# Moving operands placed 256 bytes away from stationary ones, modulo 512, in a two-block kernel on one core

## What is computed

```
first_block, for each of 2 layers:
    h = h + hybrid_mixer(rmsnorm(h))            # ends in y @ w_mix_out
    h = h + cross_attention(rmsnorm(h), mem)    # x @ w_xq, mem @ w_xkv, o @ w_xo
    layer 0:  h = h + swiglu(hn, w_gate, w_up, w_down)             # inner width 2816
    layer 1:  h = h + moe_swiglu(hn, ...)      # 8 experts of inner width 3584, top 2 of 8
second_block: mLSTM and LRU branches, two merges, then a lookup of 16 rows
    for each of 8 heads of each token in a table of 16384 experts
```

## Time and profile before

| what | value |
|---|---|
| median of three runs | 2800.35 us |
| the profiled execution | 2810.22 us |
| its span, first to last instruction | 2808.5 us |
| TensorE busy | 93% of the span |
| VectorE busy | 71% |
| ScalarE busy | 42% |
| mean granted TensorE clock | 0.968 of full speed |
| bytes moved by DMA | 776.22 MB |

### The profile page before, as it was taken

One profiled execution on the slowest core, in us unless ns is written; L12 is line 12 of the kernel. 1 busy time (PEld: TensorE's weight loads), 2 busy tenths in 40 slices (PEclk: granted clock), 3 DMA queues, 4 the chain that ended last, 5 costly groups with the idle time before them and its releaser, 6 DMA issues.

```text
span 2808.5 us, 33021 instructions
## 1 busy us (share of the span) xinstructions
PE 2612.0 (93%) x12361; PEld 2042.8 (73%) x12361; DVE 2006.7 (71%) x2922; ACT 1188.8 (42%) x1220; POOL 253.3 (9%) x281
## 2 busy tenths in 40 slices
PE   9989999999899999999999999998998997887887
PEld 7888998798788888888888888887886543333332
DVE  4775553874798888889898886446515887788775
ACT  1444332253577777778677775123401110111010
POOL 0000000000000000000000000000001433333331
PEclk9999999999899999999999999999998999998989
DMA  6543554540699999999999996642546999999997
GB/s 206 163 134 109 181 181 131 162 136 31 246 354 346 352 351 338 363 333 370 332 352 352 351 352 238 186 120 75 165 150 240 393 421 421 421 421 422 421 421 313
DMA packets 335917, 776.22 MB, mean 276 GB/s; under 512 B 21952, under 2 KB 154176, under 8 KB 302784
## 3 DMA queue, kind: packets, MB, share of 16 engines
q1 hardware_dynamic: 298080, 503.94, 51.5%
q0 software_dynamic: 36864, 268.45, 23.1%
q10 hardware_dynamic: 864, 2.38, 0.2%
HBM read 773.67 MB, written 1.05 MB: 276 GB/s over the span
## 4 chain that ended last, share of the span: by engine, by line
PE 77%; DMA 12%; DVE 8%; issue 2%; ACT 1%; DVEq 0%; POOL 0%; ACTq 0%; POOLq 0%
DMA dense_weights<-in_peer_rows,work 12%; PE banks L751 12%; PE banks L753 12%; PE banks L752 11%; PE banks L570 9%; PE banks L629 5%; PE banks L1122 5%; PE banks L592 4%; PE banks L593 4%; PE banks L596 4%; PE banks L1085 2%; PE banks L514 1%; DVE dense_weights L2422 1%; PE banks L898 1%; PE banks L814 1%
## 5 line engine op out<-in xcount | busy, mean ns | idle before, releaser
L2075 DVE TENSOR_TENSOR weight_tiles_low<-weight_tiles,weight_tiles_high 128x2048 fp32r<-128x2048 f32 x334 | 758.9, 2289 | 126.0 <-ACT weight_tiles_high L1553 124.6
L1553 ACT ACTIVATE weight_tiles_high<-weight_tiles 128x2048 fp32r<-128x2048 f32 x332 | 634.8, 1917 | 172.1 <-DMA weight_tiles<-in_moe_w_down 91.3
L1122 PE MATMUL banks<-dense_weights,work 128*128 128x512 f32 x952 | 469.8, 647 | 111.4 <-DVE work L2432 111.0
L1122 PEld LDWEIGHTS banks<-dense_weights,work 128*128 128x128 f32 x952 | 191.0, 206 | 378.7 <-issue 219.9
L751 PE MATMUL banks<-weight_tiles_high,gathered_parts 128*128 128x512 f32 x896 | 355.2, 396 | 0.8 <-ACT squares L1548 0.8
L753 PE MATMUL banks<-weight_tiles_high,gathered_parts 128*128 128x512 f32 x896 | 350.5, 391 | 0.0
L752 PE MATMUL banks<-weight_tiles_low,gathered_parts 128*128 128x512 f32 x896 | 349.7, 390 | 0.0
L2422 DVE CUSTOM_DVE_ANT_0 dense_weights<-dense_weights,banks 128x1024 f32<-128x1024 f32 x238 | 286.3, 1218 | 88.1 <-DMA dense_weights<-in_peer_rows,work 86.6
L1337 POOL DMA_INDIRECT dense_weights<-in_peer_rows,work x238 | 224.9, 945 | 737.6 <-DVE work L2391 366.6
L1743 ACT ACTIVATE work<-work 128x2 f32<-128x2 f32 x129 | 26.2, 203 | 562.4 <-DVE work L2422 560.1
L1800 DVE TENSOR_TENSOR weight_tiles_low<-weight_tiles,weight_tiles_high 128x2048 fp32r<-128x2048 f32 x73 | 166.9, 2290 | 135.7 <-ACT weight_tiles_high L1358 134.7
(11 more groups left out here) (392 smaller groups left out, 3809.6 us busy)
## 6 DMA issues: line engine op xcount, KB each, us to landing
weight_tiles<-in_moe_w_gate SPq DMA_DIRECT2D x112, 1024.0 KB, 5.1
weight_tiles<-in_moe_w_up SPq DMA_DIRECT2D x112, 1024.0 KB, 5.2
weight_tiles<-in_moe_w_down SPq DMA_DIRECT2D x112, 1024.0 KB, 4.8
weight_tiles<-in_w_in SPq DMA_DIRECT2D x38, 1024.0 KB, 5.7
weight_tiles<-in_w_xkv SPq DMA_DIRECT2D x16, 1024.0 KB, 5.5
weight_tiles<-in_ffn_w_gate SPq DMA_DIRECT2D x11, 1024.0 KB, 5.3
weight_tiles<-in_ffn_w_up SPq DMA_DIRECT2D x11, 1024.0 KB, 5.4
weight_tiles<-in_ffn_w_down SPq DMA_DIRECT2D x11, 1024.0 KB, 4.8
```

Of the source, the lines that this page charges most:

```text
L1122: mm = pe.matmul(halves[half], diag[(first + j) % 8], pair_row(first + j)[:, 1, half * 512:(half + 1) * 512], start=False, stop=end and j ...
L1553: act.activation(high_tile(j), raw_tile(j), ACT.Copy).then_inc(g.high, 1)
L2075: dve.tensor_tensor(low_tile(j), raw_tile(j), high_tile(j).bitcast(F32), ALU.subtract).then_inc(g.split, 1)
```

## The change

The change moves no instruction and adds none: on each of the five engines the list of instructions, with their shapes and names, is the same. Only addresses differ. `weight_tiles_high` becomes 64 floats longer, and the `x_high` in it begins 64 floats later; everything that is allocated behind it shifts by 256 bytes. `gathered_parts` becomes 64 floats longer as well, so that everything behind it shifts by 512 bytes in all. Inside `work_parts` the starts of `he_high`/`he_low`, of `y_low`/`mem_high` and of `o_low`/`hid_high`/`hid_low` move by 16 or 48 floats.

```
+X_HIGH_AT, XE_AT = 64, 0
+HE_AT, Y_AT, HID_AT = 5392, 7696, 16
...
-        low_tiles, high_tiles = (sb(f"weight_tiles_{x}", [P, RING, TILE_F], F32R) for x in ("low", "high"))
+        low_tiles, high_flat = sb("weight_tiles_low", [P, RING, TILE_F], F32R), sb("weight_tiles_high", [P, RING * TILE_F + X_HIGH_AT], F32R)
+        high_tiles = high_flat[:, 0:RING * TILE_F].rearrange("p (s f) -> p s f", s=RING)
...
-        xe_parts = sb("gathered_parts", [P, 2, KT, P], F32R)
+        xe_flat = sb("gathered_parts", [P, 2 * KT * P + 64], F32R)
+        xe_parts = xe_flat[:, XE_AT:XE_AT + 2 * KT * P].rearrange("p (a k s) -> p a k s", a=2, k=KT)
...
-        yF = view(7648, KT, SEQ)
+        yF = view(Y_AT, KT, SEQ)
...
-        x_high, x_low = by_k(high_tiles[:, 6, :]), xe_parts[:, :, :, :].rearrange("p a k s -> p (a k s)").rearrange("p (k s) -> p k s", k=KT)
-        mem_high, mem_low = by_k(work_parts[:, 9696:9696 + KT * SEQ]), by_k(high_tiles[:, 3, :])
-        y_low, o_low = by_k(work_parts[:, 7648:7648 + KT * SEQ]), by_k(work_parts[:, 0:KT * SEQ])
-        hid_high, hid_low = (work_parts[:, i * FT * SEQ:(i + 1) * FT * SEQ].rearrange("p (f s) -> p f s", f=FT) for i in range(2))
+        X_AT = 6 * TILE_F + X_HIGH_AT
+        x_high, x_low = by_k(high_flat[:, X_AT:X_AT + KT * SEQ]), by_k(xe_flat[:, 0:KT * SEQ])
+        mem_high, mem_low = by_k(work_parts[:, Y_AT + KT * SEQ:Y_AT + 2 * KT * SEQ]), by_k(high_tiles[:, 3, :])
+        y_low, o_low = by_k(work_parts[:, Y_AT:Y_AT + KT * SEQ]), by_k(work_parts[:, HID_AT:HID_AT + KT * SEQ])
+        hid_high, hid_low = (work_parts[:, HID_AT + i * FT * SEQ:HID_AT + (i + 1) * FT * SEQ].rearrange("p (f s) -> p f s", f=FT) for i in range(2))
...
-        he_high, he_low = (work_parts[:, 5376 + i * EXP_W:5376 + (i + 1) * EXP_W].rearrange("p (a b) -> p a b", b=P) for i in range(2))
-        he_all = view(5376 + EXP_W, ET, P)
-        ye = view(12544, D)
+        he_high, he_low = (work_parts[:, HE_AT + i * EXP_W:HE_AT + (i + 1) * EXP_W].rearrange("p (a b) -> p a b", b=P) for i in range(2))
+        he_all = view(HE_AT + EXP_W, ET, P)
+        ye = view(HE_AT + 2 * EXP_W, D)
```

## The result

The change did not make the kernel faster. Its median is 2807.53 us (20 runs, 2802.11 to 2815.64), beside 2801.43 us for the kernel before, measured beside it (20 runs, 2795.41 to 2811.03). The ratio is 1.0019, with a 95% interval of 1.0010 to 1.0028: slightly slower by an interval that leaves 1 out, and still inside the 0.2% that the prediction called no change. The prediction was 2744 us, with a range of 2722 to 2785: wrong.

The account below looks back on a forecast made before the run. The prediction took TensorE's matmul pitch as the bound: 19.9 us outside the experts plus 38.4 in them, less 2 for stalls, gave 56.3 us off 2810.2, or 2753.9; less 9.9 for the median of runs, 2744 us, range 2722 to 2785.

Parts of the forecast that it names:

- The reading of the bound: Feed-forward layer and experts, 1178 us of 2808.5: the end is set by how fast TensorE's matmuls follow each other.
- Continued to 256 it gives 111.6 ns: 256-column split matmuls: excess falling 2.1 ns per 64 bytes of distance, extended to 256, leaves an excess of 2.5 ns.
- the 19.9 us outside the experts: Summed gain claimed for queries, keys and values, mixer and attention outputs, and the feed-forward products.
- The floor of a split matmul is then 109.1 ns for 256 columns and 215.7 ns for 512.: All split matmuls at full clock: lowest possible pitch, taken from plain float32 with 2.4 ns unavoidable.
- excess: A split matmul's pitch above its assumed floor; 11.5 ns in the experts' gate and up, 10.9 in feed-forward gate and up.
- 38.4 us: Gain claimed in the experts: 24.2 us in gate and up, 14.2 us in down, at 218.2 ns a matmul.
- The row that did not fit: Experts' down product, 512 columns at distance -192: 228.8 ns, slightly worse than the 227.2 at distance 0.
- The distance doesn't matter: Rival, all split matmuls: something other than operand distance makes the excess; time 2800 us, chance 0.07.
- The slower rival: All split matmuls: signed distance counts and 256 costs 13.1 ns excess or more; time 2817 us, chance 0.10.
- 12.6 us for 256 columns: Slower case's loss: 2.2 ns on 1952 matmuls at distance 0, 4.2 on 640 at 64, 8.5 on 656 at 192.
- 4.3 us in the experts: Slower case's loss in the experts' gate and up products: 1.6 ns on 2688 matmuls.
- Costed at nothing: Terms priced at 0: plain float32 products, already at their floor, and `mem_low`, which stays at distance 0.

Follow-up runs that it names:

- exp32: Changed kernel with the experts' stationary operands 32 bytes further, nothing else moved; 2829.00 us, ratio 1.0089 to the kernel before.
- at192: Changed kernel with all moving activations of the 256-column products except `mem_low` at distance 192; 2787.52 us, ratio 0.9946 to the kernel before.
- sweep1: Bare fp32r matmul program, no kernel: operand distance stepped by 32 bytes to 512; at distance 0, 120.0 ns for 256 columns, 226.7 for 512.
- he_only: Kernel before with only `he_high` and `he_low` moved from 192 to 256; 2801.55 us beside 2802.49, ratio 0.9997.
- sweep4: Bare matmul program, no kernel: distance in single floats, fewer columns loaded, plain float32, different entry distances; 113.3 to 123.3 ns for 256 columns loading 128.
- sweep2: Bare fp32r matmul program, no kernel: operands in nine pairs of partition regions, eight distances each; all pairs alike, 113.3 to 120.0 ns for 256 columns.

## Why the prediction was wrong

- **The reading of the bound held.** TensorE's pitch sets the time in the feed-forward layer and in the experts: 0.26 us more a chunk came out as 21.5 us in `exp32`, 6.7 ns less a matmul as 20 us in `at192`. Loads and VectorE were never the limit. That the distance between the operands moves the pitch held too: `sweep1`, `at192` and `exp32` each show it. The rule of the Trainium skill that the prediction set beside it (TensorE: Matmul & The Clock Gate, "Step-by-step: what each phase is for"), that the weight load takes no bandwidth from the running matmul, agrees with the bf16 and plain float32 blocks, and does not fit fp32r, whose pitch changes with the distance (113.3 to 123.3 ns).
- **The step that failed: "Continued to 256 it gives 111.6 ns".** Three points at 0, 64 and 192 were joined by a line of 2.1 ns for 64 bytes and the line was drawn on to 256. The pitch is no line: it jumps from float to float, between 113.3 and 123.3, and it repeats every 256 bytes, so that at 256 it is that of 0 again, 120.0 ns. The prediction had evidence only that it repeats at 512 "at most". With this the 19.9 us outside the experts became a loss of about 6, since 1296 matmuls left 64 and 192 for a distance that is as slow as 0, and the others, at 0 before, gained nothing.
- **The second: "The floor of a split matmul is then 109.1 ns for 256 columns and 215.7 ns for 512."** That was taken from plain float32 products, another type, and with a wrong reading: the 64 rows are 32 matmuls, since each leaves two rows, so that a plain product of 256 columns costs 431.6 ns and not the 213.3 and 2.4 of the prediction. bf16 does reach 109.2 and 215.8; fp32r was never seen below 113.3 and 226.7. So of the 11.5 ns of "excess" in gate and up nothing could be gained by a distance, and 38.4 us, two thirds of the sum, were not there to be had: gate and up stayed at 226.7, and down went from 228.8 to 226.7 for 1344 matmuls, 1.5 us in `he_only` and 1.9 after the change.
- **The row that did not fit was the warning.** The down product at -192 was slower than gate and up at 0, in the width that carried most of the gain, and the prediction kept its line "because 256 and -256 are the same distance". Modulo 256, -192 is 64, and the sweeps have 228.8 to 229.0 there.
- **The rivals.** "The distance doesn't matter" named nearly the right time for a wrong reason. The slower rival had the right side and the right place, 256 no better than 0, but its pitch of 122.2 was too high: at 120.0 nothing at distance 0 loses, and of its 12.6 us for 256 columns 5.9 stay (656 x 6.6 and 640 x 2.4), less where TensorE waits or runs at the lower clock; its 4.3 us in the experts did not come.
- Costed at nothing, and so measured: the plain float32 products (215.8 ns from row to row in the kernel before and after), and the keys' matmuls with `mem_low` (120.0 after, as at distance 0).

## What to carry to other kernels

Before an address is moved, sweep the distance in a bare loop with the kernel's own type, width and loading: it takes one short program, and a line through three points found in different stages had the wrong period and the wrong shape. Take the floor from the same type, never from a neighbour: the gain that can be had is the present pitch less the lowest pitch of that sweep. For fp32r here that meant 6.7 ns for 256 columns at a distance of 192 bytes, worth 0.5% of the time, and nothing for 512 columns at 0. Then read the pitch of each loop in the kernel's own trace, since one distance can have two: 192 gave 117.8 in the attention output of `at192`.

## What the runs showed of the hardware

- The pitch of fp32r matmuls with 128 columns loaded depends on the distance between moving and stationary operand, modulo 256 bytes, and changes with a step of one float: 113.3 to 123.3 ns at 256 columns, 226.7 to 240.0 at 512 (`sweep4`). bf16 (109.2, 215.8) and plain float32 (215.8 and 429.2 for each of the two rows of a matmul) were the same at the four distances tried. The place of either operand in the partition didn't count (`sweep2`), nor which of them is displaced except for the sign (`sweep1`).
- At one distance there can be two stable pitches (113.3 and 117.8 at 192, 113.3 and 118.6 at 16), by what ran before; so a sweep of one order gives one of the values that a distance can have. Distance 112 gave 113.3 in each of the three sweeps that had it. And behind an interruption 512 columns take about ten steps at 231 ns before they settle at 226.7.
- At the lower clock, 1.2 GHz (granted clock 0.50), the two stretches looked at show no such difference: 213.8 ns at distance 0, and 213.3 in the values of the memory from 156.74 us on in the kernel before, which cost 117.8 at the full clock. No other distance was measured there.
- Why fp32r has a floor 4.1 and 10.9 ns above bf16, and what picks the mode, stays open: the runs show the dependence and not its cause.
